# Output projection tile 0 started before the third head's transposes, and the fifth key chunk split before the squares of the memory

## The reference

```python
def rmsnorm(x, g):
    y = x * lax.rsqrt(jnp.mean(x * x, axis=-1, keepdims=True) + EPS)
    return y * g

def mem_attention(h, m, w_q, w_kv, w_o):          # h: 512 x 1024, m = rmsnorm(mem, g): 256 x 1024
    q = (h @ w_q).reshape(B, S, 4, 256)
    k, v = jnp.split(m @ w_kv, 2, axis=-1)         # each (B, 256, 4, 256)
    scores = jnp.einsum('bshd,bnhd->bhsn', q, k) * 256 ** -0.5
    p = jax.nn.softmax(scores, axis=-1)
    o = jnp.einsum('bhsn,bnhd->bshd', p, v).reshape(B, S, D)
    return o @ w_o
```

## Time and profile before

| | |
|---|---|
| median of 3 runs | 1147.44 us (1147.26 to 1147.80) |
| the profiled execution | 1147.92 us, span 1146.0 us |
| PE busy | 1132.5 us, 99% |
| DVE, ACT, POOL busy | 815.6, 648.9, 207.0 us |
| granted clock of PE | 0.999 of full speed |
| instructions | 16195 |

### The profile page before, as it was taken

How to read it: one execution, slowest core, us unless ns; L and a number is a source line. 1 busy time by engine, 2 the same in 40 slices (tenths; PEclk the granted TensorE clock), 3 DMA queues, 4 the chain that set the end, 5 groups by cost and what they waited for, 6 DMA issues and landing times.

```text
span 1146.0 us, 16195 instructions
## 1 busy us (share of the span) xinstructions
PE 1132.5 (99%) x6556; PEld 998.9 (87%) x6556; DVE 815.6 (71%) x931; ACT 648.9 (57%) x803; POOL 207.0 (18%) x192
## 2 busy tenths in 40 slices
PE   9999999999999999999999999999999999999997
PEld 7988888998999999888888888888999999998985
DVE  7887646786786786886488645664668678677688
ACT  6764445775565655655444443444586666556665
POOL 0040013113012121122264012001211211112110
PEclk9999999999999999999999999999999999999999
DMA  9532133899789778755232632313389977977855
GB/s 351 214 91 94 56 130 74 175 272 195 193 179 203 185 143 185 163 108 199 79 103 80 217 98 74 107 41 147 74 201 245 201 189 176 210 175 150 182 103 136
DMA packets 49290, 177.65 MB, mean 155 GB/s; under 512 B 5568, under 2 KB 5952, under 8 KB 48576
## 3 DMA queue, kind: packets, MB, share of 16 engines
q0 software_dynamic: 18976, 68.17, 33.0%
q1 hardware_dynamic: 28656, 104.35, 27.3%
q10 hardware_dynamic: 1584, 4.10, 1.0%
HBM read 173.45 MB, written 2.10 MB: 153 GB/s over the span
## 4 chain that ended last, share of the span: by engine, by line
PE 90%; DVE 6%; ACT 2%; issue 1%; DMA 1%; POOL 0%; SPq 0%; DVEq 0%; POOLq 0%; ACTq 0%
PE psum L2006 12%; PE psum L2007 12%; PE psum L2008 12%; PE psum L2266 9%; PE psum L2268 9%; PE psum L2267 9%; PE psum L2286 8%; PE psum L2287 8%; PE psum L2288 8%; DMA w_raw<-in_weights 1%; PE psum L2203 1%; DVE w_lo L1259 1%; PE psum L2325 1%; DVE w_lo L1248 1%; POOL sq L1995 0%
## 5 line engine op out<-in xcount | busy, mean ns | idle before, releaser
L2286 PE MATMUL psum<-w_lo,slot_hi 128*128 128x512 f32 x448 | 175.3, 391 | 0.3
L2287 PE MATMUL psum<-w_hi,slot_hi 128*128 128x512 f32 x448 | 174.8, 390 | 0.0
L2288 PE MATMUL psum<-w_hi,slot_lo 128*128 128x512 f32 x448 | 174.3, 389 | 0.0
L1259 DVE TENSOR_TENSOR w_lo<-w_sum,w_hi 128x1024 fp32r<-128x1024 f32 x96 | 116.9, 1223 | 65.2 <-ACT w_hi L756 65.1
L2266 PE MATMUL psum<-xs_s_lo,w_hi 128*128 128x256 f32 x512 | 145.4, 284 | 0.9 <-issue 0.9
L2268 PE MATMUL psum<-xs_s_hi,w_lo 128*128 128x256 f32 x512 | 144.8, 283 | 0.0
L2267 PE MATMUL psum<-xs_s_hi,w_hi 128*128 128x256 f32 x512 | 144.8, 283 | 0.0
L756 ACT ACTIVATE w_hi<-w_sum 128x1024 fp32r<-128x1024 f32 x96 | 101.2, 1055 | 69.6 <-PE psum L2288 56.4
L1259 DVE TENSOR_TENSOR w_lo<-w_raw,w_hi 128x1024 fp32r<-128x1024 f32 x80 | 97.6, 1223 | 41.6 <-ACT w_hi L756 41.3
L756 ACT ACTIVATE w_hi<-w_raw 128x1024 fp32r<-128x1024 f32 x80 | 83.8, 1055 | 71.7 <-PE psum L2268 51.5
L2268 PE MATMUL psum<-xs_a_hi,w_lo 128*128 128x256 f32 x384 | 108.7, 283 | 0.0
(11 more groups left out here) (236 smaller groups left out, 2706.3 us busy)
## 6 DMA issues: line engine op xcount, KB each, us to landing
w_raw<-in_weights SPq DMA_DIRECT2D x89, 512.0 KB, 3.7
w_sum<-in_down POOLq DMA_DIRECT2D x52, 512.0 KB, 7.3
w_raw<-in_up POOLq DMA_DIRECT2D x48, 512.0 KB, 7.2
w_sum<-in_down SPq DMA_DIRECT2D x44, 512.0 KB, 4.7
w_raw<-in_up SPq DMA_DIRECT2D x32, 512.0 KB, 3.9
up<-in_up SPq DMA_DIRECT2D x16, 512.0 KB, 4.5
up<-in_up POOLq DMA_DIRECT2D x16, 512.0 KB, 7.5
up<-in_down POOLq DMA_DIRECT2D x12, 512.0 KB, 6.2
```

What stands on the lines that cost most here:

```text
L1259: dve.tensor_tensor(w_lo[:, c % RING, :], buffer(kind, b, SUM_BUFFER[STAGE[p][0]] + half), w_hi[:, c % RING, :].bitcast(F32), ALU.subtract ...
L2286: pe.matmul(to, s_hi[:, k, tok], w_lo[:, c % RING, cols], start=first, stop=False, skip_group_check=True)
L2287: pe.matmul(to, s_hi[:, k, tok], w_hi[:, c % RING, cols], start=False, stop=False, skip_group_check=True)
L2288: last = pe.matmul(to, s_lo[:, k, tok], w_hi[:, c % RING, cols], start=False, stop=(kp == 1 and j == 1), skip_group_check=True)
```

## The change

At the start, ACT and DVE split chunk 4 before the squares and before the tree of sums; PE's four sums follow chunk 4 instead of chunk 3. In attention, of both layers, the first product of output tile 0 (three matmuls) goes ahead of head 2's transposes in step 4; one product more of tile 1 goes ahead of head 3's transposes in its place; and one product of tile 0 is moved from behind head 3's values to ahead of them. The number of instructions is the same, and so is the bank of each result.

```diff
             hi_weights(3)
+            hi_weights(4)
             act.activation(mem_sq[:], mem0_raw[:], ACT.Square).then_inc(memsq_ready, 1)
-            hi_weights(4)
             hi_weights(5)
@@
             lo_weights(3)
+            lo_weights(4)
             trees = 0
             dve.wait_ge(memsq_ready, 1)
             for n in (4, 2, 1):
...
-            lo_weights(4)
             lo_weights(5)
@@
                 kv_chunk(C["k0"] + k, "k0", k, mem0_hi, mem0_lo)
-                if k == 3:
+                if k == 4:
                     pe.wait_ge(tree_step, 3)
                     sums("stat_mem", NT, squares=mem_sq)
@@
                 for h in range(HEADS + 1):
                     if h < HEADS:
                         q_tile(2 * h)
+                    else:
+                        out_part(0, 0, 1)
                     if h >= 2:
                         transposes(h - 2)
@@
-                out_part(0, 0, 4)
-                out_part(1, 0, 1)
+                out_part(0, 1, 4)
+                out_part(1, 0, 2)
                 transposes(HEADS - 1)
-                out_part(1, 1, 4)
+                out_part(1, 2, 4)
+                out_part(0, 4, 5)
                 values(HEADS - 1)
-                for first, end in ((4, 6), (6, 8)):
-                    for m in range(2):
-                        out_part(m, first, end)
+                out_part(0, 5, 6)
+                out_part(1, 4, 6)
+                for m in range(2):
+                    out_part(m, 6, 8)
```

## The result

| | before | changed |
|---|---|---|
| median of 22 runs each | 1147.64 us | 1149.57 us (1149.07 to 1151.03) |
| ratio | | 1.0017 (95% interval 1.0011 to 1.0022) |
| span of the profiled execution | 1146.0 us | 1148.0 us |

The kernel became 1.93 us slower. The forecast was +1.3, 1148.7 in 1147.3 to 1150.0, on the slow side and within 0.2%.

What follows compares the result with a forecast made beforehand. PE bounds the kernel, busy 1132.5 of 1146.0 us, so only its idle time or work matters. Start -0.4 plus attention +1.7 gives +1.3 on the median 1147.44: 1148.7, range 1147.3 to 1150.0.

Steps and rivals of the forecast that it cites:

- The bank (part 2): Attention, each layer: PE stands at output tile 0's bank until DVE's low part; loss 0.85, upper bound 0.93.
- the shortened cover at the end of attention: Behind head 3's values: nine matmuls of cover instead of twelve, low part still hidden by 1.2; cost nothing.
- The start (part 1): Chunk 4 split ahead of the squares: its 0.72 wait goes; gain 0.4, bounds -0.1 (a loss) and 0.8.
- the wait at chunk 6: Start: PE newly waits ahead of chunk 6 for its late low part, giving back 0.35 to 0.85.
- The root ran quietly: Start: DVE's root steps assumed near the quiet root's pace, mostly clear of POOL's casts; 1.25 from mean_sq to chunk 6.
- The sum: Whole kernel: -0.4 + 1.7 = +1.3, bounds +0.9 and +2.0; no measurable change, on the slow side.
- (a): Attention rival: the bank is free in time and the hole is filled; -1.8, 1145.7; chance 0.12.
- (b): Start rival: late low parts from chunk 6 on reach PE again, at pool or y tiles; 1149.6 to 1150.3; chance 0.08.
- DVE's lateness from chunk 6 on: DVE runs 0.9 late after the start, with 1.00 idle ahead of 44.25; costed at nothing.
- (c): Attention rival: PE's clock falls to 1.2 GHz behind the 1.8 wait in each layer; 1153.5; chance 0.05.
- What would show it: Trace signs: waits naming value tiles' low part, about 1.8; scores 3.4 after values; chunk 4 wait gone, 0.3 to 0.8 at chunk 6.

Runs made afterwards that it cites:

- wait_alone: Kernel before, no work moved; PE only waits for output tile 0's bank ahead of head 2's transposes, both layers: 1149.52 us, +1.75 (1.0015).
- attn_free_bank: Changed kernel with the start as before and a bank plan that keeps a long-taken bank for output tile 0, against the kernel before: 1146.31 us, -1.33 (0.9988).
- bank_control: Kernel before in its old order of work, with only the new plan of banks: 1147.82 us, +0.05 (1.0001).
- changed_look_1: The changed kernel unaltered, a second profiled single execution: 1149.23 us, span 1147.3.
- attn_only: Attention part of the change alone, the start as before, against the kernel before: 1149.49 us, +1.85 (1.0016).
- start_only: Start part of the change alone, attention as before, against the kernel before: 1147.39 us, -0.25 (0.9997).
- start_pool_first: Start part alone, and DVE waits for POOL's last addition between its first and second weight splits, against the kernel before: 1147.56 us, -0.08 (0.9999).

## Why the prediction was right, and where its sum was off

**The bank (part 2): right.** The step that decided the sign was that the moved piece brings its bank's wait to a place where the bank isn't free, though no row of the old trace shows PE at it. `wait_alone`, `attn_free_bank` and `bank_control` together show it: the wait alone costs 1.75, a free bank turns +1.85 into -1.33, the plan alone does nothing. The forecast of 0.85 a layer (upper bound 0.93) measured 1.85 / 2 = 0.92 in time and 3.42 - 1.85 - 0.68 = 0.89 in the trace. The 0.04 in the trace are the step from DVE's end to PE's start, for which I took 0.06; it was 0.10. The other 0.03 is less than the times can tell. Nothing downstream took it back, as forecast; the shortened cover at the end of attention cost nothing.

**The start (part 1): the mechanism right, the wait at chunk 6 too long, the gain in time smaller.** The wait at chunk 4 went and a shorter one came at chunk 6. That one was 0.14 instead of the forecast 0.35 to 0.85. The lower end was built from 1.25 for the root and 0.14 from DVE's end to PE's start, and PE ready 3.15 after the start of the sums. Measured were 1.20 (22.59 to 23.79), 0.06 (25.07 to 25.13) and 3.23 (21.76 to 24.99), which leaves 0.14. Counted from the end of chunk 3, chunk 7 started at 28.83 - 19.34 = 9.49 before and at 27.98 - 19.04 = 8.94 in the changed kernel: 0.55 gained, not 0.4.

The root ran quietly, as assumed: the step that took 0.52 beside POOL's cast took 0.16. The casts were over at 22.48, where I had derived 23.2 from the rule in the Trainium skill's "SBUF — State Buffer", "Who interferes with whom". The rule isn't what was off: POOL's first cast ended 0.54 after the end of DVE's split of chunk 5 (21.93 and 21.39), before the change 0.52 after it (22.14 and 21.62), and in `changed_look_1`, with the split over by 21.16, it took 0.67 alone. So the 0.83 of the earlier trace rows, which I used as its price, already held a wait for DVE, and the traces fit a full block.

```profile
20.11 1.28 DVE L1248 SCALAR_TENSOR_TENSOR w_lo<-w_raw,gains,w_hi 128x1024 fp32r<-128x1024 f32 x1
22.59 0.16 DVE L1302 TENSOR_SCALAR mean_sq<-psum 128x2 f32<-128x2 f32 x1 [1.20 <-ACT sd_mem L775]
...
23.06 0.16 DVE L1291 TENSOR_TENSOR root_t<-root_t,mean_sq 128x2 f32<-128x2 f32 x1
...
23.79 2.48 DVE L1248 SCALAR_TENSOR_TENSOR w_lo<-w_raw,gains,w_hi 128x1024 fp32r<-128x1024 f32 x2
...
20.93 1.00 POOL L1926 CAST band_hi<-band_raw 128x576 fp32r<-128x576 f32 x1 [20.48 <-DMA band_raw<-in_band]
```

The same cast in `changed_look_1`, with no split beside it:

```profile
21.36 0.67 POOL L1927 CAST band_hi<-band_raw 128x576 fp32r<-128x576 f32 x1 [20.91 <-DMA band_raw<-in_band]
```

Over all profiled executions, the last matmul of head 1's values in layer 0 starts at 135.59 on average in the five kernels with the old start, and at 135.16 in the six executions with the new one and no blocked addition: 0.43 gained. That it is so near the forecast 0.4 is partly luck: those six ended chunk 3, which the change doesn't touch, 0.12 later on average than the five (19.37 for 19.25). Counted from there, the gain is 0.55 again. In the medians it is 0.25, 0.08 and 0.33, and between `attn_only` and the changed kernel, from different sets of runs, -0.08, a loss. One reason is seen: the blocked addition, at 85.9, gave back all of it and more in one execution (135.84 in the changed kernel's profile). How often it does isn't settled: it was one of the five profiles in which it could happen. Nothing shows it to be more frequent in the changed kernel than in `start_only`, to which it is identical up to that point, and the differences in question, 0.2 to 0.3, are near what these sets of runs can tell apart. That stays open.

**The sum.** +1.7 became +1.85; -0.4 became something between -0.3 and +0.1. The forecast +1.3 measured +1.93, and 0.2 of the distance between 1148.7 and 1149.57 is the kernel before itself, whose median over 22 runs is 1147.64 and not 1147.44. So +1.93 came out close to the upper bound, +2.0: the bank's term was right, and the start's gain, the term that was off, hardly showed in the medians. The forecast took 0.2% for the least that can be told from no change; with 22 runs each the interval, 1.0011 to 1.0022, tells 0.17%.

**Rivals.** (a), the filled hole, didn't happen, and is what `attn_free_bank` is; its 0.68 a layer was right. (b), the start giving back more, happened in part (the start's gain doesn't show in the changed kernel's median) but not by its mechanism: DVE's lateness from chunk 6 on was absorbed ahead of the tokens' root, where it still idled (0.17 of the 1.00 in the earlier trace rows). In the profiled execution the place that gave back was one I hadn't priced, POOL's sum at 85.9, because the old trace has no wait there. (c), the clock: the longest wait in the old trace is not that of 0.6 for the probabilities but 1.46 at the very start, so 1.8 wasn't twice the longest. In any case the clock held: the window around the wait of 1.70, in the changed kernel (us, engines' busy time with instructions, granted clock, DMA), has it at 1.00, and so has the next.

```profile
135.00:138.00 3.00, 1.30 (x7) 0.79 (x5) 2.09 (x7) 1.86 (x6) 0.00 (x0) 1.00 0.13 49
138.00:142.00 4.00, 4.00 (x32) 3.82 (x33) 2.43 (x5) 1.09 (x2) 0.00 (x0) 1.00 0.02 4
```

**What would show it.** Right: the place and length of the wait, the scores at 3.4, the wait at chunk 6. Wrong: that the list would name the value tiles' low part. It says "issue". Only the row of DVE that ends 0.10 before PE starts, or `wait_alone`, tells who it was.

## What to carry to other kernels

Before a piece of work is moved into a hole of an in-order queue, write down every semaphore that the piece waits for, and look in the other engines' rows for when each was raised, its output buffer's included; the old trace shows no wait for a buffer that was asked for late enough. If the buffer is the obstacle, plan another one first: here that turned a loss of 1.85 us into a gain of 1.33 with the same instructions. And where a gain makes an engine earlier, look for the next place at which it meets another engine with little to spare, not only for the next wait that the old trace shows.

## What the hardware showed that was not expected

Two engines' overlapping elementwise work, DVE's three splits and POOL's addition, was slowed in either of two ways, in executions of the same program: DVE by about 1.1 (4.58 against 3.48) with POOL's addition at 2.17, or POOL to 4.44 with DVE at 3.48. Both were through after nearly the same time, 4.58 (81.99 to 86.57) and 4.62 (81.15 to 85.77); which engine pays differs, and it was worth 1.0 us of PE's time. The rule that the two exclude each other, in the Trainium skill's "SBUF — State Buffer", "Who interferes with whom", agrees with both: POOL's addition ended 1.15 after the first split's end or 1.14 after the third's. What decides between the two wasn't found.

With the new start, lateness at the very start stays. From the end of chunk 3 to the last matmul of head 1's values, the six executions without a blocked addition took 115.78 to 115.80: `start_pool_first`, which had waited 1.2 for the memory's second piece, ended chunk 3 at 19.69 and was at 135.49, `start_only` at 19.21 and 134.99. With the old start, where PE waits at chunk 4 for DVE, the same stretch took 116.18 to 116.60. Whether part of the lateness is forgiven there isn't shown.
